# Attention in a one-core transformer block: the two heads or halves of a tile issued together on TensorE

## The chip, the cores and the metric

The program runs on one NeuronCore of one Trainium2 chip. The metric is the device time of one execution in microseconds. Three executions of the kernel before gave 3341.49, 3347.58 and 3352.87 us, median 3347.58.

## What is computed

One transformer block on two groups of tokens with shared weights: 1024 tokens (on a grid of 16 rows of 64) and 256 tokens. The reference, cut to what matters here:

```python
h = rms_norm(x, mix_norm_w)
qa, ka, va, qd, kd, vd = split(h @ w_in, 6)          # 6 x 512 columns
# neighbourhood attention: 8 heads of 64, window of 8 grid rows x 16 columns, learned bias
s = qg @ kg * 64**-0.5 + bias;  s = where(in_window, s, -inf)
ya = rms_norm(softmax(s) @ vg)                       # per head
# differential attention: 4 heads, q and k in two halves c of 64, v of 128, T5 bias
s = einsum('bqhcd,bkhcd->bhcqk', q, k) * 64**-0.5 + bias
p = softmax(s);  a = p[:, :, 0] - lam * p[:, :, 1]
yb = rms_norm(a @ v) * (1 - lambda_init)             # per head
x = x + concat(ya, yb) @ w_out
x = x + expert_choice_ffn(rms_norm(x))               # 16 experts, each token row routed
return rms_norm(x)
```

## The kernel before

The program has one written-out instruction order per engine; semaphores tie the engines together. Its stages, in order: normalisation and projection of V; four neighbourhood jobs (NA, two heads of 64 each); projection of V for the differential heads; four differential jobs (DF, one head with two halves of 64 each); the output projection; the router; sixteen experts; the final normalisation. Attention lies between 153 and 905 us of the profiled span.

A job works on the ten query tiles of 128 tokens (`TT`), tiles 0 to 7 of the long group and 8 and 9 of the short one. An NA tile has a window of 512 keys (t = 0, 1, 6, 7), 576 keys (t = 2 to 5, in two chunks of 288) or 256 keys (t = 8, 9); a DF tile has 1024 keys in two chunks of 512, or 256. A *unit* is one head or half of one tile, so there are twenty (`UNITS`) in a job. The two heads or halves sit in partitions 0 to 63 and 64 to 127 of `qk_h` and `qk_l`, which are the rounded value and the rest of q and k. The scores of one chunk of a unit are three matmuls over 64 rows (`three`, L542 to L544: high with high, low with high, high with low) into one half of the PSUM tensor `S`, which has one half for each of two units. Then:

- VectorE adds the bias, negates, writes the result to a slot of `E` in SBUF and takes its minimum (`bias_max`, L1215). It increments `scores_read`, which frees that half of `S`.
- ScalarE takes the exponential in place (`exps`, L937).
- In DF, VectorE then mixes the two halves (`mix`: a reciprocal L1257, a factor L1259, the mixing L1263).
- TensorE turns the blocks of 128 columns (`turn`, L537) into one of the two banks of `PT`, up to four blocks to a *fill*; a fill waits until the fill two before it is copied. ScalarE copies each fill to `PTs` (`turned_copy`, L924).
- TensorE multiplies with `Vj` (`na_values`, L598; `values`, L589) into `O` or `G`. In NA ScalarE copies that to `oTs` (L966), TensorE turns it once more, and ScalarE takes squares and copies it to `o_all` (`na_out`, L953 and L955). In DF ScalarE does it without the turn (`out_copy`, L932 and L933).

The order of NA on TensorE (L625 to L649) is by units: in step s the scores of unit s, the turns of unit s-2, the values of unit s-3, and in odd steps the turn of an output. The scores of a unit wait until the unit two before it has been read. ScalarE in step s: `na_out`, the copies of unit s-2, `oTs`, the exponential of unit s (L957 to L972). `w_round` (L880, ScalarE) and `w_lows` (L1136, VectorE) split the weights of the next job's projection after unit 8. Four projection rounds (`project`, rounded by `proj_round` and `proj_lows`) follow the attention of each job but the last DF job, with the last turns and values between them.

The order of DF on TensorE (`df_body`, L668) is by tiles: scores of both halves of tile t, values of t-2, turns of t-1, which wait for the mixing of t-1. VectorE: bias of half 0 of t, mixing of t-1, bias of half 1 of t. `E` has four slots, two for each of two tiles. GpSimd scales the finished heads and stores them (`heads`, `heads_scale`).

## Time and profile before

| | us |
|---|---|
| median of three runs | 3347.58 |
| span of the profiled execution | 3352.0 |
| its own time beside the span | not given apart from the span |
| TensorE busy (matmul) | 2967.7 (89%) |
| VectorE busy | 2059.2 (61%) |
| ScalarE busy | 1846.5 (55%) |
| GpSimd busy | 1355.1 (40%) |
| granted clock, mean of the span | 0.939 |

### The profile page before, as it was taken

How to read it: one execution, taken by the hardware profiler on the slowest of the kernel's cores; microseconds unless marked ns; L12 is line 12 of the kernel's file. 1: busy time of each engine (PE TensorE's matmuls, PEld its weight loads, DVE VectorE, ACT ScalarE, POOL GpSimd, SP SyncE). 2: the span in 40 equal slices, each digit the busy share in tenths (PEclk: the TensorE clock that was granted, in tenths of full speed). 3: DMA queues.
4: the chain of work that ended last, by engine and by line, in shares of the span. 5: the costliest groups of instructions: out<-in, count | busy, mean ns of one | idle time of the engine just before them, and what ended most of it. 6: DMA issues, size and time to landing. Idle time of an engine off the chain costs nothing.

```text
span 3352.0 us, 63730 instructions
## 1 busy us (share of the span) xinstructions
PE 2967.7 (89%) x23200; PEld 2709.3 (81%) x23200; DVE 2059.2 (61%) x2651; ACT 1846.5 (55%) x3280; POOL 1355.1 (40%) x1107
## 2 busy tenths in 40 slices
PE   3999999889698399898998999989989999899894
PEld 3877778777576298898988989889889898898894
DVE  3222223444533787786776867768768677687784
ACT  2144441444411176676665766756657667576674
POOL 1112211110211164564653745636447356374473
PEclk9999999999799599999999999999999999999997
DMA  6211100101235298998989989989899898898996
GB/s 157 75 25 32 45 32 21 33 28 31 83 126 176 65 298 252 274 271 250 289 256 246 296 250 281 264 243 303 250 265 278 254 278 263 246 300 248 274 273 215
DMA packets 790984, 657.24 MB, mean 196 GB/s; under 512 B 28311, under 2 KB 771863, under 8 KB 790263
## 3 DMA queue, kind: packets, MB, share of 16 engines
q1 hardware_dynamic: 778539, 608.52, 62.7%
q0 software_dynamic: 12240, 45.52, 5.2%
q8 instruction: 185, 3.03, 0.4%
q14 instruction: 20, 0.16, 0.0%
HBM read 618.58 MB, written 39.62 MB: 196 GB/s over the span
## 4 chain that ended last, share of the span: by engine, by line
PE 77%; issue 11%; DVE 5%; ACT 3%; DMA 2%; POOL 1%; DVEq 0%; SPq 0%; ACTq 0%; POOLq 0%
PE S L799 24%; PE S L802 11%; PE G L799 7%; PE S L542 6%; PE S L544 5%; PE S L543 5%; PE O L799 5%; PE PT L537 3%; PE G L802 3%; PE O L802 2%; DMA w_st<-in_w_in_dram 1%; PE O L598 1%; PE G L598 1%; ACT wh L1057 1%; DVE E L1215 1%
## 5 line engine op out<-in xcount | busy, mean ns | idle before, releaser
L1427 DVE TENSOR_TENSOR wl<-stg,wh 128x2048 bf16<-128x2048 f32 (+1 forms) x482 | 1260.3, 2617 | 323.0 <-ACT wh L1057 321.8
L799 PE MATMUL S<-X,wh 128*128 128x320 f32 x5632 | 940.3, 321 | 91.4 <-issue 86.7
L1057 ACT ACTIVATE wh<-stg 128x2048 fp32r<-128x2048 f32 (+1 forms) x482 | 1004.5, 2084 | 0.2
L799 PEld LDWEIGHTS S<-X,wh 128*128 128x128 f32 x5632 | 854.7, 194 | 98.9 <-issue 98.6
L1681 POOL TENSOR_TENSOR hx<-hh,hx 128x160 fp32r<-128x160 f32 x352 | 413.6, 1175 | 348.0 <-ACT hx L1089 347.7
L1683 POOL CAST hb<-hx 128x160 bf16<-128x160 f32 x352 | 549.0, 1560 | 0.0
L802 PE MATMUL S<-Xb,wl 128*128 128x160 bf16 x5632 | 454.7, 235 | 0.0
L802 PEld LDWEIGHTS S<-Xb,wl 128*128 128x128 bf16 x5632 | 385.0, 99 | 36.7 <-issue 1.4
L799 PE MATMUL O<-hx,wh 128*128 128x320 f32 x1408 | 229.8, 317 | 49.5 <-POOL hb L1683 49.5
L799 PEld LDWEIGHTS O<-hx,wh 128*128 128x128 f32 x1408 | 208.7, 190 | 54.0 <-POOL hx L1681 52.3
L799 PE MATMUL G<-hx,wh 128*128 128x320 f32 x1408 | 246.3, 336 | 0.0
L937 ACT ACTIVATE E<-E,nmax 128x1024 f32<-128x1024 f32 (+3 forms) x160 | 137.8, 861 | 176.7 <-DVE nmax L1215 176.7
L799 PEld LDWEIGHTS G<-hx,wh 128*128 128x128 f32 x1408 | 231.1, 209 | 0.7
L1575 POOL TENSOR_TENSOR ca<-lsum,half 128x20 f32<-128x20 f32 (+3 forms) x9 | 22.9, 2547 | 466.4 <-ACT o_all L933 342.9
L1663 POOL CAST Xb<-X 128x320 bf16<-128x320 f32 x68 | 109.7, 1625 | 211.5 <-ACT X L1047 211.5
L537 PE MATMUL PT<-identf,E 128*128 128x128 f32 x640 | 105.9, 300 | 94.5 <-DVE E L1175 49.6
L1074 ACT ACTIVATE glo<-S 128x160 f32<-128x160 f32 x352 | 87.4, 300 | 167.5 <-PE S L802 165.5
L537 PEld LDWEIGHTS PT<-identf,E 128*128 128x128 f32 x640 | 75.9, 150 | 120.6 <-issue 87.9
L1690 POOL DMA_INDIRECT residual<-ye,idx_c x16 | 25.9, 1619 | 361.0 <-ACT yes L1098 361.0
L1204 DVE SCALAR_TENSOR_TENSOR qk_l<-S,qk_h 128x1024 fp32r<-128x1024 f32 (+1 forms) x32 | 26.4, 825 | 214.4 <-ACT qk_h L912 214.4
L924 ACT ACTIVATE PTs<-PT 128x512 f32<-128x512 f32 (+2 forms) x184 | 87.0, 507 | 127.1 <-PE PT L537 126.8
L1462 DVE TENSOR_TENSOR hh<-sg,uu 128x160 f32<-128x160 f32 x352 | 114.9, 326 | 65.2 <-DVE uu L1457 61.3
(225 smaller groups left out, 4604.5 us busy)
## 6 DMA issues: line engine op xcount, KB each, us to landing
stg<-in_w_gate_dram SPq DMA_DIRECT2D x177, 1024.0 KB, 5.5
stg<-in_w_up_dram SPq DMA_DIRECT2D x177, 1024.0 KB, 5.6
stg<-in_w_down_dram SPq DMA_DIRECT2D x128, 1408.0 KB, 13.4
w_st<-in_w_in_dram SPq DMA_DIRECT2D x16, 512.0 KB
yt<-mixed SPq DMA_DIRECT2D x10, 512.0 KB, 3.8
residual<-x2t POOLq DMA_DIRECT2D x10, 512.0 KB, 4.4
ffn_in<-h2t POOLq DMA_DIRECT2D x10, 512.0 KB, 4.0
fin<-residual SPq DMA_DIRECT2D x10, 512.0 KB, 8.3
```

The lines of the kernel that those rows point to most:

```text
L537: mm = pe.transpose(PT[:, bank, m * P:(m + 1) * P], src(b), identf[:, :])
L542: pe.matmul(out, lhs_h, rhs_h, start=first, stop=False)
L543: pe.matmul(out, lhs_h, rhs_l, start=False, stop=False)
L544: return pe.matmul(out, lhs_l, rhs_h, start=False, stop=last)
L799: pe.matmul(out, w, x, start=first, stop=False, skip_group_check=True)
L802: return pe.matmul(out[:, 0:CT], w, x, start=False, stop=last, skip_group_check=True)
L937: act.activation(E[:, slot, 0:nk], E[:, slot, 0:nk], ACT.Exp, scale=-1.0, bias=nmax[:, col:col + 1], accum_out=lsum[:, job(j), t, c:c + 1] ...
L1057: act.activation(wh[:, kk % NCV, 0:w], stg[:, kk % NST, 0:w], ACT.Copy).then_inc(rounded, 1)
L1427: dve.tensor_tensor(wl[:, kk % NCV, 0:w], stg[:, kk % NST, 0:w], wh[:, kk % NCV, 0:w].bitcast(F32), ALU.subtract).then_inc(split, 1)
L1462: dve.tensor_tensor(hh[:, m, :], sg[:, m, :], uu[:, m, :], ALU.mult).then_inc(hidden_made, 1)
L1681: pool.tensor_tensor(hx[:, f, CT:2 * CT], hh[:, f % 2, :], hx[:, f, 0:CT].bitcast(F32), ALU.subtract).then_inc(hidden_ready, 1)
L1683: pool.tensor_copy(hb[:, f, :], hx[:, f, 0:CT].bitcast(F32)).then_inc(hidden_b, 1)
```

## The change

NA goes by tiles instead of units. On TensorE step s holds the scores of both heads of tile s, the values of both heads of tile s-2, the turns of both heads of tile s-1, and the turn of the output of tile s-3. Within the scores the three matmuls of a chunk alternate between the two heads (rows 0 to 63, rows 64 to 127), each head in its own half of `S`; within the values the blocks alternate between the two heads (columns 0 to 63, columns 64 to 127). The scores now wait until both heads of the tile before have been read. ScalarE in step s: both exponentials of tile s, `oTs` of tile s-2, `na_out` of tile s-4, the copies of tile s-1. `w_round` moves to the end of step 4, `w_lows` to after unit 11.

In DF the scores of the two halves alternate in the same way. The turns are those of tile t-2 and stand before the values, which are those of tile t-3. VectorE does both biases of tile t and then the mixing of t-1. A fifth slot `E5`, over the tables of NA, makes three slots for half 0, in turn by tile (`df_E`). The order of the projection rounds among the last turns and values changes with it.

```diff
     turns, outs, f = [], [], 0
-    for s in range(STEP):
-        if 2 <= s < UNITS + 2:
-            turns.append(f)
-            f += -(-na_blocks((s - 2) // 2) // 4)
-        if s % 2 and s >= 5:
+    for s in range(1, TT + 3):
+        if s <= TT:
+            for _ in range(2):
+                turns.append(f)
+                f += -(-na_blocks(s - 1) // 4)
+        if s >= 3:
             outs.append(f)
             f += 1
...
+    E5 = at("E5", [P, 1024], F32, 160 * K)
...
+    def df_E(t, c):
+        return E[:, 2 + t % 2, :] if c else (E[:, 0, :], E[:, 1, :], E5[:, :])[t % 3]
...
-            def scores(n, u, t, hf, k0, chunks):
-
-                pe.wait_ge(scores_read, n - 1)
-                rows = slice(64 * hf, 64 * hf + 64)
+            def scores(n, t, k0, chunks):
+
+                pe.wait_ge(scores_read, n)
                 q = slice(t * P, (t + 1) * P)
                 for at_, key, ln in chunks:
                     kk = slice(k0 + key, k0 + key + ln)
-                    mm = three(S[:, u % 2, at_:at_ + ln], qk_h[rows, 0, q], qk_l[rows, 0, q],
-                               qk_h[rows, 1, kk], qk_l[rows, 1, kk], True, True)
-                mm.then_inc(scores_ready, 1)
+                    for w, (qs, ks) in enumerate(((qk_h, qk_h), (qk_l, qk_h), (qk_h, qk_l))):
+                        for hf in range(2):
+                            rows = slice(64 * hf, 64 * hf + 64)
+                            mm = pe.matmul(S[:, hf, at_:at_ + ln], qs[rows, 0, q], ks[rows, 1, kk],
+                                           start=(w == 0), stop=(w == 2))
+                            if w == 2 and key + ln == chunks[-1][1] + chunks[-1][2]:
+                                mm.then_inc(scores_ready, 1)
 
             def values(o, par, fills_done, blocks, lhs, rhs, cols):
                 pe.wait_ge(turned_copied, fills_done)
...
-            def na_values(i, t, hf, fills_done, keys, kt0):
+            def na_values(i, t, fills_done, keys, kt0):
 
                 pe.wait_ge(turned_copied, fills_done)
                 pe.wait_ge(oT_copied, i * TT + (t + 1))
                 for b, n in enumerate(keys):
-                    mm = pe.matmul((O, G)[t % 2][64 * hf:64 * hf + 64, 0:P],
-                                   Vj[0:n, kt0 + b, 64 * hf:64 * hf + 64], PTs[0:n, hf, b, :],
-                                   start=(b == 0), stop=(b == len(keys) - 1))
-                mm.then_inc(out_ready, 1)
+                    for hf in range(2):
+                        mm = pe.matmul((O, G)[t % 2][64 * hf:64 * hf + 64, 0:P],
+                                       Vj[0:n, kt0 + b, 64 * hf:64 * hf + 64], PTs[0:n, hf, b, :],
+                                       start=(b == 0), stop=(b == len(keys) - 1))
+                        if b == len(keys) - 1:
+                            mm.then_inc(out_ready, 1)
 
 
...
                 n0, f0 = i * STEP + U_NA, i * NA_F
...
                         chunks = [(0, 0, 288), (512, 288, 288)] if inner else [(0, 0, nk)]
-                        scores(n0 + s, s, s // 2, s % 2, kt0 * P, chunks)
+                        scores(n0 + 2 * s, s, kt0 * P, chunks)
+                    elif s == TT:
+                        pe.wait_ge(w_split, i + (W_QKN + 1))
+                        project(n0 + UNITS, 0)
+                    elif s == TT + 1:
+                        project(n0 + UNITS, 1)
+                        project(n0 + UNITS, 2)
                     else:
-                        if s == UNITS:
-                            pe.wait_ge(w_split, i + (W_QKN + 1))
-                        project(n0 + UNITS, s - UNITS)
-                    if 2 <= s < UNITS + 2:
-                        u = s - 2
-                        pe.wait_ge(exp_done, i * UNITS + (u + 1))
-                        turn((f0, F_NA + NA_TURN[u]), list(range(na_blocks(u // 2))),
-                             lambda b: E[:, u % 4, b * P:(b + 1) * P])
-                    if 3 <= s < UNITS + 3:
-                        u = s - 3
-                        kt0, nk, _, _ = na_window(u // 2)
-                        if u == 0:
+                        project(n0 + UNITS, 3)
+                    if 2 <= s < TT + 2:
+                        t = s - 2
+                        kt0, nk, _, _ = na_window(t)
+                        if t == 0:
                             pe.wait_ge(vj_ready, i + 1)
-                        keys = [min(P, nk - b * P) for b in range(na_blocks(u // 2))]
-                        na_values(i, u // 2, u % 2, f0 + (F_NA + na_turned(u)), keys, kt0)
-                    if s % 2 and s >= 5:
-                        t = (s - 5) // 2
+                        keys = [min(P, nk - b * P) for b in range(na_blocks(t))]
+                        na_values(i, t, f0 + (F_NA + na_turned(2 * t + 1)), keys, kt0)
+                    if 1 <= s < TT + 1:
+                        for u in (2 * s - 2, 2 * s - 1):
+                            pe.wait_ge(exp_done, i * UNITS + (u + 1))
+                            turn((f0, F_NA + NA_TURN[u]), list(range(na_blocks(u // 2))),
+                                 lambda b: E[:, u % 4, b * P:(b + 1) * P])
+                    if s >= 3:
+                        t = s - 3
                         pe.wait_ge(oT_copied, i * TT + (t + 3))
                         turn((f0, F_NA + NA_OUT[t]), [t % 2], lambda b: oTs[:, b, :])
 
             v_project(W_VB, U_V1)
             v_project(W_VB + 1, U_V1 + TT)
 
-            def df_scores(n0, t, c):
+            def df_scores(n0, t):
                 k0, nk = df_keys(t)
-                scores(n0 + (2 * t + c), c, t, c, k0, [(a, a, min(512, nk - a)) for a in range(0, nk, 512)])
+                scores(n0 + 2 * t, t, k0, [(a, a, min(512, nk - a)) for a in range(0, nk, 512)])
 
             def df_turn(i, t):
                 pe.wait_ge(mixed, i * TT + (t + 1))
                 turn((i * DF_F, F_DF + df_fills(t)), list(range(df_keys(t)[1] // P)),
...
                         pe.wait_ge(vj_ready, i + (JOBS + 1))
                     if t >= 2:
-                        df_values(i, t - 2)
-                    if t >= 1:
-                        df_turn(i, t - 1)
+                        df_turn(i, t - 2)
+                    if t >= 3:
+                        df_values(i, t - 3)
                 if not last:
                     pe.wait_ge(w_split, i + (W_QKD + 1))
                     project(n0 + UNITS, 0)
+                df_turn(i, TT - 2)
+                df_values(i, TT - 3)
+                if not last:
+                    project(n0 + UNITS, 1)
+                    project(n0 + UNITS, 2)
                 df_turn(i, TT - 1)
                 df_values(i, TT - 2)
                 if not last:
-                    project(n0 + UNITS, 1)
-                    project(n0 + UNITS, 2)
+                    project(n0 + UNITS, 3)
                 df_values(i, TT - 1)
-                if not last:
-                    project(n0 + UNITS, 3)
 
 
             with pe.Fori(0, JOBS - 1) as i:
...
-                        na_out((s - 6) // 2)
-                    if 2 <= s < UNITS + 2:
-                        u = s - 2
-                        turned_copy(f0, F_NA + NA_TURN[u], i * UNITS + u, u % 2, na_blocks(u // 2))
-                    if s % 2 and s >= 5:
-                        t = (s - 5) // 2
+                for s in range(TT + 4):
+                    if s < TT:
+                        exps(i, n0 + 2 * s, E[:, 2 * s % 4, :], na_window(s)[1], 2 * s, s, 0)
+                        exps(i, n0 + 2 * s + 1, E[:, (2 * s + 1) % 4, :], na_window(s)[1], 2 * s + 1, s, 1)
+                    elif s == TT:
+                        proj_round(n0 + UNITS, 0)
+                    elif s == TT + 1:
+                        proj_round(n0 + UNITS, 1)
+                        proj_round(n0 + UNITS, 2)
+                    elif s == TT + 2:
+                        proj_round(n0 + UNITS, 3)
+                    if 2 <= s < TT + 2:
+                        t = s - 2
                         act.wait_ge(out_ready, i * UNITS + (2 * t + 4))
                         act.activation(oTs[:, t % 2, :], (O, G)[t % 2][:, 0:P], ACT.Copy).then_inc(oT_copied, 1)
-                    if s < UNITS:
-                        exps(i, n0 + s, s % 4, na_window(s // 2)[1], s, s // 2, s % 2)
-                    elif s < STEP:
-                        proj_round(n0 + UNITS, s - UNITS)
-                    if s == 8:
+                    if 4 <= s < TT + 4:
...
+                    if s == 4:
                         w_round(W_QKN, i)
 
...
 
                 for t in range(TT):
                     nk = df_keys(t)[1]
+                    for c in range(2):
+                        exps(i, n0 + (2 * t + c), df_E(t, c), nk, 2 * t + c, t, c)
                     if t >= 2:
                         tcopy(t - 2)
-                    exps(i, n0 + 2 * t, 2 * (t % 2), nk, 2 * t, t, 0)
                     if t == 3:
                         act.wait_ge(heads_normed, i + (JOBS + 1))
                     if t >= 3:
                         ocopy(t - 3)
-                    exps(i, n0 + (2 * t + 1), 2 * (t % 2) + 1, nk, 2 * t + 1, t, 1)
...
-                    if s == 8:
+                    if s == 11:
...
+                    if t >= 3:
+                        dve.wait_ge(turned, i * DF_F + (F_DF + df_fills(t - 2)))
+                    elif t == 0:
+                        dve.wait_ge(turned, i * DF_F + F_DF)
+                    if t >= 2:
+                        dve.wait_ge(mixed, i * TT + (t - 1))
                     for c in range(2):
-                        if t >= 2:
-                            dve.wait_ge(turned, i * DF_F + (F_DF + df_fills(t - 1)))
-                        else:
-                            dve.wait_ge(turned, i * DF_F + (F_DF - DF_F + df_fills(TT + t - 1)))
-                        slot = 2 * (t % 2) + c
                         bias_max(n0 + (2 * t + c), c, S[:, c, 0:nk],
                                  BT[:, (TPR - 1) * P - tl * P:(TPR - 1) * P - tl * P + nk],
-                                 E[:, slot, 0:nk], 2 * t + c)
-                        if c == 0 and t >= 1:
-                            mix(i, t - 1)
+                                 df_E(t, c)[:, 0:nk], 2 * t + c)
+                    if t >= 1:
+                        mix(i, t - 1)
```

TensorE in NA, in the middle of the four tiles of 576 keys: before, the end of one unit's scores, then turns and values, each of one head (the line in brackets names the semaphores that an instruction waits for; `S<-qk_h 128x288` is a chunk of scores, `PT<-identf,E` a turn, `O<-PTs,Vj` values).

```order
L542 MATMUL S<-qk_h 128x288
L543 MATMUL S<-qk_l,qk_h 128x288
L544 MATMUL S<-qk_h,qk_l 128x288
L636 REGISTER_ALU
L533 REGISTER_ALU [waits exp_done]
L537 MATMUL PT<-identf,E 128x128 [waits turned_copied]
L537 MATMUL PT<-identf,E 128x128 x3
L533 REGISTER_ALU
L537 MATMUL PT<-identf,E 128x128 [waits turned_copied]
L598 MATMUL O<-PTs,Vj 64x128 [waits oT_copied,turned_copied]
L598 MATMUL O<-PTs,Vj 64x128 x4
L648 REGISTER_ALU
```

The same place in the change (L588 is the scores' matmul, L607 the values').

```order
L588 MATMUL S<-qk_h 128x288 [waits scores_read]
L588 MATMUL S<-qk_h 128x288
L588 MATMUL S<-qk_h,qk_l 128x288 x2
L588 MATMUL S<-qk_l,qk_h 128x288 x2
L588 MATMUL S<-qk_h 128x288 x2
L588 MATMUL S<-qk_h,qk_l 128x288 x2
L588 MATMUL S<-qk_l,qk_h 128x288 x2
L603 REGISTER_ALU
L607 MATMUL O<-PTs,Vj 64x128 [waits oT_copied,turned_copied]
L607 MATMUL O<-PTs,Vj 64x128 x9
L657 REGISTER_ALU
L542 MATMUL PT<-identf,E 128x128 [waits turned_copied,exp_done]
```

The scores of a tile are twelve matmuls in a row with one wait, the values ten, and the turns stand behind them.

ScalarE in NA, one unit before: output of an earlier tile, the two copies of a turned unit, the exponential.

```order
L950 REGISTER_ALU [waits turned_copied]
L953 ACTIVATE junk,sso<-PT 128x64 [waits turned]
L953 ACTIVATE junk,sso<-PT 128x64
L955 ACTIVATE o_all<-PT 128x128
L923 REGISTER_ALU [waits out_ready]
L924 ACTIVATE PTs<-PT 128x512 [waits turned]
L923 REGISTER_ALU
L924 ACTIVATE PTs<-PT 128x128 [waits turned]
L936 REGISTER_ALU
L937 ISA [waits scores_read]
L937 ACTIVATE E,lsum<-E,nmax 128x576
```

The change, from the second exponential of a tile on (L952 is the exponential, L986 `oTs`, L968 and L970 the output, L939 the copies).

```order
L951 REGISTER_ALU
L952 ISA [waits scores_read]
L952 ACTIVATE E,lsum<-E,nmax 128x576
L986 ACTIVATE oTs<-G 128x128 [waits out_ready]
L965 REGISTER_ALU [waits turned_copied]
L968 ACTIVATE junk,sso<-PT 128x64 [waits turned]
L968 ACTIVATE junk,sso<-PT 128x64
L970 ACTIVATE o_all<-PT 128x128
L938 REGISTER_ALU [waits out_ready]
L939 ACTIVATE PTs<-PT 128x512 [waits turned]
L938 REGISTER_ALU
L939 ACTIVATE PTs<-PT 128x128 [waits turned]
```

The copies have moved from before the exponential to behind both exponentials, `oTs` and the output.

VectorE in DF, before: the bias of half 0 of tile t, the mixing of tile t-1 (L1257 to L1263), the wait for the bias of half 1.

```order
L1215 ISA E,nmax<-S,BT 128x1024 [waits scores_ready]
L1215 ISA nmax 128x1
L1256 REGISTER_ALU
L1257 ISA [waits exp_done]
L1257 RECIPROCAL rl_88<-lsum 128x1
L145 REGISTER_ALU
L1259 ISA [waits dve_own]
L1259 TENSOR_SCALAR cf<-rl_88,lsum,lam_s 128x1
L145 REGISTER_ALU
L1263 SCALAR_TENSOR_TENSOR E<-E,cf 128x1024 [waits dve_own]
L1213 REGISTER_ALU [waits turned]
L1215 ISA E,nmax<-S,BT 128x1024 [waits scores_ready]
```

The change, from the wait ahead of tile 2 on (L1236 is the bias, L1278 and L1280 lead to the mixing).

```order
L1234 REGISTER_ALU [waits mixed]
L1236 ISA E_65,nmax<-S,BT 128x1024 [waits scores_ready]
L1236 ISA nmax 128x1
L1234 REGISTER_ALU
L1236 ISA E,nmax<-S,BT 128x1024 [waits scores_ready]
L1236 ISA nmax 128x1
L1277 REGISTER_ALU
L1278 ISA [waits exp_done]
L1278 RECIPROCAL rl_89<-lsum 128x1
L146 REGISTER_ALU
L1280 ISA [waits dve_own]
L1280 TENSOR_SCALAR cf<-rl_89,lsum,lam_s 128x1
```

Both biases stand ahead of the mixing; the wait on `mixed` is new.

## Rows read from the trace of the kernel before

**Rows 1.** Of the page: the chain that ended last, by engine

```profile
PE 77%; issue 11%; DVE 5%; ACT 3%; DMA 2%; POOL 1%; DVEq 0%; SPq 0%; ACTq 0%; POOLq 0%
```

**Rows 2.** Sums by stretch: start and end, length, busy time (instructions), clock, DMA

```profile
sum 226.40, PE 219.03 PEld 159.56 DVE 66.57 ACT 137.88 POOL 42.90; mean PE 54.76 PEld 39.89 DVE 16.64 ACT 34.47 POOL 10.72
...
564.00:649.95 85.95, 75.87 (x459) 63.34 (x457) 41.70 (x76) 38.92 (x92) 1.48 (x1) 0.96 0.08 25
649.95:741.20 91.25, 79.90 (x458) 67.05 (x457) 44.44 (x76) 39.41 (x93) 11.49 (x10) 0.91 0.10 29
741.20:831.40 90.20, 79.08 (x458) 66.35 (x457) 44.43 (x76) 39.29 (x93) 11.44 (x10) 0.92 0.06 18
831.40:905.00 73.60, 55.09 (x313) 45.79 (x312) 49.40 (x78) 42.16 (x90) 17.00 (x17) 0.84 0.23 75
```

**Rows 3.** Timeline, TensorE in an NA tile: start, busy us, engine, line, operation

```profile
264.36 0.40 PE L542 MATMUL S<-qk_h 64*128 64x288 f32 x1
264.60 0.29 PE L543 MATMUL S<-qk_l,qk_h 64*128 64x288 f32 x1
264.73 0.29 PE L544 MATMUL S<-qk_h,qk_l 64*128 64x288 f32 x1
267.42 0.33 PE L537 MATMUL PT<-identf,oTs 128*128 128x128 f32 x1
267.68 0.40 PE L542 MATMUL S<-qk_h 64*128 64x288 f32 x1
```

**Rows 4.** Timeline, VectorE and ScalarE in the same stretch (in brackets: idle, and its releaser)

```profile
262.55 0.76 DVE L1215 CUSTOM_DVE_ANT_0 E<-S,TI 128x576 f32<-128x576 f32 x1 [2.55 <-PE S L544]
264.39 1.91 ACT L880 ACTIVATE w_h<-w_st 128x2048 fp32r<-128x2048 f32 x1
266.33 2.29 DVE L1136 TENSOR_TENSOR w_l<-w_st,w_h 128x2048 fp32r<-128x2048 f32 x1 [3.02 <-ACT w_h L880]
269.42 0.78 ACT L937 ACTIVATE E<-E,nmax 128x576 f32<-128x576 f32 x1 [2.31 <-DVE nmax L1215]
270.74 0.81 ACT L924 ACTIVATE PTs<-PT 128x512 f32<-128x512 f32 x2
271.45 0.77 ACT L937 ACTIVATE E<-E,nmax 128x576 f32<-128x576 f32 x1
```

**Rows 5.** Timeline, a DF tile: TensorE and VectorE

```profile
606.97 0.50 PE L542 MATMUL S<-qk_h 64*128 64x512 f32 x1
607.31 0.40 PE L543 MATMUL S<-qk_l,qk_h 64*128 64x512 f32 x1
607.55 0.61 PE L542 MATMUL S<-qk_h 64*128 64x512 f32 x2
608.81 1.22 DVE L1215 CUSTOM_DVE_ANT_0 E<-S,BT 128x1024 f32<-128x1024 f32 x1 [1.85 <-PE S L544]
608.82 0.39 PE L544 MATMUL S<-qk_h,qk_l 64*128 64x512 f32 x1
610.57 1.28 DVE L1263 SCALAR_TENSOR_TENSOR E<-E,cf 128x1024 f32<-128x1024 f32 x1
611.98 1.09 PE L537 MATMUL PT<-identf,E 128*128 128x128 f32 x8 [0.57 <-DVE E L1263]
```

**Rows 6.** Timeline, TensorE at the scores of the first short DF tile

```profile
613.00 0.43 PE L542 MATMUL S<-qk_h 64*128 64x256 f32 x2
```

**Rows 7.** Two slices round the rounding of an NA job's weights

```profile
178.00:181.00 3.00, 1.40 (x11) 1.04 (x11) 1.26 (x4) 2.29 (x10) 0.00 (x0) 1.00 0.00 0
181.00:184.00 3.00, 3.00 (x13) 2.23 (x11) 0.00 (x0) 0.60 (x2) 0.00 (x0) 0.51 0.00 0
```

**Rows 8.** Timeline, VectorE in the first tiles of the second DF job

```profile
658.51 2.17 DVE L1263 SCALAR_TENSOR_TENSOR E<-E,cf 128x1024 f32<-128x1024 f32 x1
667.23 1.22 DVE L1215 CUSTOM_DVE_ANT_0 E<-S,BT 128x1024 f32<-128x1024 f32 x1
```

**Rows 9.** Timeline, the first projection matmul behind the first DF job

```profile
621.07 0.47 PE L542 MATMUL S<-hT_h,w_h 128*128 128x512 f32 x1
```

More of the change, by code:

```diff
@@ L955, in na_out @@
                     act.activation(o_all[:, t, :], PT[:, bank, 0:P], ACT.Copy).then_inc(turned_copied, 1)
-                for s in range(STEP + 1):
-                    if s % 2 == 0 and s >= 6:
-                        na_out((s - 6) // 2)
-                    if 2 <= s < UNITS + 2:
-                        u = s - 2
-                        turned_copy(f0, F_NA + NA_TURN[u], i * UNITS + u, u % 2, na_blocks(u // 2))
-                    if s % 2 and s >= 5:
-                        t = (s - 5) // 2
+                for s in range(TT + 4):
+                    if s < TT:
+                        exps(i, n0 + 2 * s, E[:, 2 * s % 4, :], na_window(s)[1], 2 * s, s, 0)
[9 more added lines that the diff above has]
+                        t = s - 2
                         act.wait_ge(out_ready, i * UNITS + (2 * t + 4))
                         act.activation(oTs[:, t % 2, :], (O, G)[t % 2][:, 0:P], ACT.Copy).then_inc(oT_copied, 1)
-                    if s < UNITS:
-                        exps(i, n0 + s, s % 4, na_window(s // 2)[1], s, s // 2, s % 2)
-                    elif s < STEP:
-                        proj_round(n0 + UNITS, s - UNITS)
-                    if s == 8:
+                    if 4 <= s < TT + 4:
+                        na_out(s - 4)
+                    if 1 <= s < TT + 1:
+                        for u in (2 * s - 2, 2 * s - 1):
+                            turned_copy(f0, F_NA + NA_TURN[u], i * UNITS + u, u % 2, na_blocks(u // 2))
+                    if s == 4:
                         w_round(W_QKN, i)
@@ L1002, in df_body @@
                         w_round(NW + t // 2)
+                if not last:
+                    proj_round(n0 + UNITS, 0)
                 tcopy(TT - 2)
@@ L1009, in df_body @@
                 if not last:
-                    proj_round(n0 + UNITS, 1)
-                    proj_round(n0 + UNITS, 2)
+                    proj_round(n0 + UNITS, 3)
                 ocopy(TT - 1)
-                if not last:
-                    proj_round(n0 + UNITS, 3)
             with act.Fori(0, JOBS - 1) as i:
```

22 lines of the change are left out of this document (11 added, 11 removed).

## The prediction, written before the changed kernel ran

> **What bounds the kernel now.** I read the page first. TensorE is busy in 89% of the span, and the chain that ended last is 77% TensorE [rows 1]; but most of that is the experts' stage, which the change leaves alone. So I cut out the two attention stages. The four stretches in which the neighbourhood jobs (NA) attend take 226.4 us together, 56.6 each, the four differential jobs (DF, the projections between them included) 341.0 us [rows 2]. The change can touch only these 567 us.
>
> Next the timeline of a steady NA tile of 576 keys. TensorE goes from the scores of one head (64 rows) to turns, to values with 128 rows, to values with 64 rows and to scores again, with some 0.17 us lost at each change of shape and no other gap. A head with the turn of an output takes 264.36 to 267.68 = 3.32 us, one without it 0.26 less (267.42 to 267.68): 6.38 us a tile [rows 3]. ScalarE and VectorE wait there. NA is bound by TensorE.
>
> In DF it is otherwise. From scores to scores a tile takes 606.97 to 613.00 = 6.03 us [rows 5, 6], and the rows form a ring: scores, bias and maximum of half 0 (608.81), reciprocal, factor and mixing of the tile before (610.57, 1.28 us), its turns (611.98, which waited 0.57 us on that mixing), scores again. DF is bound by this ring, and no engine is full in it.
>
> **Do the two halves run together?** The diff rests on it, and before already shows it. In the two short tiles the scores of both halves stand right behind each other, and the two first matmuls show as one row of x2 that spans 0.43 us, where one alone lasts 0.38 [rows 6]. With 512 columns half 1's first matmul starts at 607.55, beside half 0's third, and before half 0's fourth (the x2 row at 607.55 spans 0.61 us) [rows 5]. Its twelve matmuls take 606.97 to 609.21 = 2.24 us. A step beside the other half is as long as alone, 0.23 to 0.24 us (607.31 to 607.55). So rows 0-63 and 64-127 overlap at full speed. Alternating, DF scores need 0.34 + 4 x 0.23 + 0.39 = 1.65 us, a gain of only 0.6. For NA scores and for the column groups of the values no row of before shows a pair: values in between nothing (20 records a tile at 0.11 us, the step of the turns, of which eight span 1.09 us [rows 5]) and half (10 slots).
>
> The Trainium skill, TensorE: Matmul & The Clock Gate, section on packing small matmuls, says that matmuls start strictly in program order. The rows at 607.55 say otherwise; by the page the scores of before would be longer by some 0.5 us, and the change worth that much more on the tiles where TensorE sets the time. I go by the rows, and no term uses it.
>
> **NA, the change part by part.** Scores of a tile: twelve matmuls become six slots; four changes of shape a tile instead of nine, at 0.17 us. TensorE's own work of a 576-key tile falls from 6.38 to about 1.0 + 1.4 + 1.4 = 3.8 us if values pair, 4.9 if not. But now `scores` waits until both halves of the tile before are read, and ScalarE does both exponentials of tile s before the copies of tile s-1, on which turns of s-1 wait, behind which stand the scores of s+1. That is a closed ring. Walked with its rows [rows 3, 4], from the start of scores(s): half 0 ready at 0.24 + 4 x 0.13 + 0.29 = 1.05; bias 0.19 later, 0.76 long: 2.00; ScalarE 0.13 later, two exponentials of 0.77: 3.67; `oTs` 0.16: 3.83; output of tile s-4 0.55 (269.42 to 270.74 less one exponential): 4.38; copy of the first fill 0.6 (both fills 0.71): 4.98; only then the second head's four turns (0.65): 5.6; their copy 0.6: 6.25; out turn and change to scores 0.3: 6.6 us. Against 6.38 that is a loss. Whether values pair matters 0.2 us to it, they lie beside ScalarE's part. The same walk gives 5.0 us for a 512-key tile in the place of some 5.3, and 3.9 and 3.5 for the two 256-key tiles. The first three tiles lack parts of the ring and take 2.5, 2.5 and 4.2, the fourth 6.0. Tiles 0 to 9: 2.5 + 2.5 + 4.2 + 6.0 + 6.6 + 6.6 + 6.25 + 5.0 + 3.9 + 3.5 = 47.1 us, and 1.3 for the second-head turns that now wait behind round 0 of the projection: 48.4.
>
> Before spends 56.6. Two things in it go. The weight rounding (1.91 us on ScalarE, then 2.29 on VectorE after a 3.02 us wait) stands in front of copies that TensorE needs [rows 4]; moved to the end of ScalarE's tile 4 it lies in 2.2 us in which ScalarE waits for bias(5), and the VectorE half after unit 11 lies in a wait for scores. Its cost: TensorE busy 1.40 of 3 us at 178, then the granted clock at 0.51 in 181-184, 1.2 GHz [rows 7]: some 2.5 us of stall and 3.4 of half clock. What is late next is the ring. And it starts slower: with TensorE under half busy in the first 5 us I expect a spell at half clock in each job, 3 us. I add 1 us for steps between engines that I left out: 52.4 a job, 209.6 in all, **-17 us**. Bounds: no spell, nothing left out, -33; half clock in all of it (scores 0.8 us longer, and the values, twice as long, stand in front of the first turn: ring 8.6, 2 us more on eight tiles, 2 in front): 66 a job, +38.
>
> The page TensorEngine Tiling (Array Packing) of the Trainium skill, section PSUM Bottleneck, warns that tiling speeds up TensorE but not the emptying of PSUM. The trace agrees for NA: 3.8 us of matmul in a ring of 6.6. By the page's other figure, up to 2x for halves of 64, NA would gain some 80 us; by the ring it can't.
>
> **DF.** The ring is cut: turns of t-2 need a mixing that ended 0.3 us or more before, thanks to the third buffer of `E`. What is late next is TensorE itself: scores 1.5, change 0.2, eight turns 0.9, sixteen value records 1.8, change 0.2 = 4.6 us. VectorE needs 2 x 1.15 + 1.81 = 4.1, ScalarE 2 x 1.15 + 1.0 + 0.5 = 3.8, and from scores to both biases read it is 1.84 + 2.31 = 4.15: all below 4.6. Start of a job: bias(2) came 667.23 - 649.95 = 17.3 us after the first scores [rows 2, 8]. Now 4.15 (scores and both biases), 2.67 (`Vj`), 2.31 (two biases): 9.1; exponential 1.28 and rounding 1.9: 12.3, beside the mixing; `w_lows` 2.3: 14.6. Then 4.15 and five times 4.6 to bias(8), less 0.85: scores(8) at 40.9, with 2 us for a spell at half clock 42.9. Two short tiles 7.5: projection at 50.4. Its part lasted 621.07 to 649.95 = 28.9 us [rows 2, 9]; turn(8) and values(7) stand in it now as well, 2.05: 30.9. Sum 81.3, in job 0, whose `Vj` copy is 1.9 us shorter, 79.4. Against 85.95, 91.25 and 90.20 [rows 2] that is -6.6, -10.0, -8.9. The last job keeps four roundings: a tile with one lasts 9.2 (ScalarE's rounding comes behind both exponentials, copy and output: 2.3 + 1.28 + 1.0 + 0.5 + 1.9 + 2.2), one without 4.6: 14.6 + 4.15 + 3 x 9.2 + 2 x 4.6 - 0.85 + 7.5 + 3.8 for what is left = 66.0 against 73.6, -7.6. Sum -33. VectorE's mixing takes 2.17 instead of 1.28 us while GpSimd works [rows 8] and may now stand in the way more often; I take 1.5 us a job off: **-27 us**. Bounds: -38 (no half clock) and -12 (TensorE's cycle at 5.3 instead of 4.6).
>
> Nothing else moves: the instructions outside these loops stand as before, the experts' stage among them; the end of the last job hangs on GpSimd's two passes over the heads, as before.
>
> **Sum.** 3352.0 - 17 - 27 = 3308 us for an execution like the profiled one, whose span is 3352.0; nothing beyond it is known of that execution's own time. The median of the three runs shown is 3347.58, 4.4 less: 3304 us.
>
> **Rivals.**
> 1. The clock in steady NA. TensorE's columns fill 4.7 of 6.4 us now, then 3.0 of 6.6. A slice with a long gap is followed by 0.51 [rows 7], which speaks for it. Against: the gaps of the new ring are spread, and both heads' columns still pass. If it swings between the levels, +5 us a job: NA +3, total -24: 3324 us. Chance 0.25.
> 2. Slower than before, by one mechanism: the ring keeps NA at half clock all through. +38 - 27 = +11: 3359 us. It decides from a mean granted clock in NA under about 0.6 (where NA's loss, 7 us a job, eats DF's gain). Before has 0.84 to 0.96 in the DF jobs [rows 2]. Chance 0.07.
> 3. The change doesn't do what it says: alternate heads with a wait or a tag between them don't pair, scores last as long as one after the other. NA's ring is 0.8 longer on eight tiles: -17 + 26 = +9. DF's cycle is 1.2 longer on five: -27 + 24 = -3. Together +6: 3354 us. The x2 row at 613.00 [rows 6] speaks against. Chance 0.06.
> The forecast keeps 0.62, its own range 3285 to 3318.
>
> **Numbers.** Range 3278 (both lower bounds make -71, 3277) to 3336 (rival 1 with DF at its poor bound). A measurement tells 0.3%, 10 us, from no change. Faster by over 0.3%: the forecast, rival 1 nearly all: 0.85. Within: part of rival 1 and rival 3: 0.08. Slower: 0.07.
>
> **What would show it.** NA stretches of 50 to 54 us, inner tiles of 6.4 to 6.8 with TensorE waiting on copies (`PT` on ScalarE L939), ScalarE without the 3 us wait round the rounding; granted clock 0.9 or more. DF tiles at 4.6 to 4.8, TensorE without waits on mixing; DF jobs near 81 and the last 66. It is wrong if NA tiles last under 6 us (a wait that I placed in the ring is not there), if DF tiles stay over 5.3, or if PEclk in NA falls below 0.8.

## The result: 14 us slower, and the profile after

The changed kernel takes 3365.86 us (median of six runs, 3363.68 to 3371.97) against 3351.86 of before (six runs, 3341.49 to 3357.72): ratio 1.0047, 95% interval 1.0031 to 1.0063. The forecast was 3304.0, range 3278 to 3336. The time is outside it, on the side that got a chance of 0.07, and not by the mechanism of that rival.

One execution of e5 (11210.75 us) and one of the kernel before beside e5, e6 and e7 (4249.48 us) were slow with unchanged code, so all figures and ratios below are of the others; the median of e5 with its slow one is 3191.84, from which the expectations of e8, e9 and e10 start.

The attention stages did what was forecast. First the sum over the four NA stretches of the changed kernel, which answers to the sum of [rows 2] (226.40 us), then its DF jobs, which answer to the four others (341.0 us; 304.83 now):

```profile
148.49:197.91 49.42, 36.70 (x312) 25.78 (x312) 15.61 (x42) 31.70 (x104) 0.00 (x0) 0.90 0.01 3
...
sum 198.71, PE 146.85 PEld 103.89 DVE 62.45 ACT 128.93 POOL 42.85; mean PE 36.71 PEld 25.97 DVE 15.61 ACT 32.23 POOL 10.71
```

```profile
541.17:620.42 79.25, 68.73 (x457) 57.58 (x457) 41.63 (x76) 38.63 (x93) 0.00 (x0) 0.96 0.09 27
620.42:701.19 80.77, 70.13 (x456) 58.56 (x456) 43.01 (x76) 38.79 (x94) 11.03 (x9) 0.92 0.11 33
701.19:780.83 79.64, 68.45 (x456) 57.28 (x457) 43.47 (x76) 38.80 (x95) 11.04 (x9) 0.94 0.06 21
780.83:846.00 65.17, 45.55 (x276) 36.99 (x277) 46.12 (x76) 38.95 (x80) 13.43 (x14) 0.75 0.25 84
```

The NA stretches end at the first projection matmul, and more of the last tiles' turns and values now stands behind it: the parts between the stretches and up to DF take 9.5 us more (193.97 against 184.45), so of the 27.7 us in the stretches 18.2 are left.

The experts' first matmul starts at 1099.8 us, where before it started at 1154.7: 54.9 us earlier (4.6 of them are the stage ahead of NA, whose time differs from run to run with unchanged code). Yet the span is 10.9 us longer, so the experts give back 66. From the first expert's first matmul to the sixteenth's the changed kernel takes 139.3 us an expert, before 135.2; 15 x 4.1 = 62 us of it lie there.

The view of the groups, TensorE's weight loads from 1100 us on, has the place. The first group is the load for the first half of an expert (columns: line, engine, operation, names, shapes, count, then busy time and mean ns, then the idle time before it and what ended it). Before:

```profile
L799 PEld LDWEIGHTS S<-X,wh 128*128 128x128 f32 x5632 | 854.7, 194 | 98.9 <-issue 98.6
```

and after, the same 5632 loads:

```profile
L814 PEld LDWEIGHTS S<-X,wh 128*128 128x128 f32 x5632 | 858.0, 194 | 158.8 <-issue 158.4
```

The instructions take the same time; 60 us more are idle, and "issue" says that the profile shows nothing that the engine waited for. On the timeline of TensorE this stands where the experts' loop (`pe.Fori(0, NE)`) goes round. Before:

```profile
1418.92 0.27 PE L861 MATMUL PT<-identf,yTe 128*32 128x128 f32 x1
1425.08 1.43 PE L799 MATMUL S<-X,wh 128*128 128x320 f32 x4 [5.88 <-issue]
```

After:

```profile
1507.45 0.27 PE L876 MATMUL PT<-identf,yTe 128*32 128x128 f32 x1
1513.58 0.63 PE L814 MATMUL S<-X,wh 128*128 128x320 f32 x1 [5.85 <-issue]
1517.41 1.97 PE L814 MATMUL S<-X,wh 128*128 128x320 f32 x6 [3.21 <-issue]
```

Both have a hole of 5.9 us at the branch. The changed kernel has a second one of 3.2 us (up to 4.2 at other turns) behind a single matmul. For the queue that carries instructions the page of before has:

```profile
q8 instruction: 185, 3.03, 0.4%
```

and after:

```profile
q8 instruction: 200, 3.28, 0.4%
```

Fifteen packets more (of 3.03 MB / 185 = 16384 bytes) for fifteen turns. In 1419 to 1430 of before that queue has 2 packets, in 1507 to 1522 of after 3:

```profile
q8 instruction: 3, 0.05, 1.3%
```

The times of these packets in the two traces tie the holes to them. In before one starts at 1422.23 and has landed at 1423.32, and TensorE goes on at 1425.08. In after one has landed at 1511.88, and TensorE goes on at 1513.58; the next starts only at 1515.18 and has landed at 1516.16, and the second hole ends at 1517.41. It is so at every turn: the first hole ends 1.7 to 1.9 us behind a landing, the second 1.2 to 1.6 us behind the next one.

The stalls cost more than their own length through the clock. In slices of 3 us (columns as in [rows 2]; the number behind the brackets is the granted clock) before has the clock at 0.50 in one slice and at 0.61 in the next:

```profile
1425.00:1428.00 3.00, 2.92 (x11) 2.93 (x12) 0.60 (x1) 0.00 (x0) 0.00 (x0) 0.50 0.87 171
1428.00:1431.00 3.00, 3.00 (x24) 2.80 (x22) 0.00 (x0) 0.00 (x0) 0.53 (x4) 0.61 0.86 281
```

After has it at 0.50 in four slices running and at 0.78 in the one behind:

```profile
1507.00:1510.00 3.00, 0.66 (x4) 0.36 (x4) 0.02 (x1) 2.82 (x6) 0.58 (x1) 0.95 0.90 273
1510.00:1513.00 3.00, 0.00 (x0) 0.00 (x0) 1.16 (x1) 1.81 (x1) 2.39 (x2) 0.50 0.76 138
1513.00:1516.00 3.00, 0.63 (x1) 0.29 (x1) 1.13 (x1) 0.00 (x0) 0.00 (x0) 0.50 0.96 174
1516.00:1519.00 3.00, 1.58 (x6) 1.59 (x7) 0.00 (x0) 0.00 (x0) 0.53 (x4) 0.50 0.88 281
1519.00:1522.00 3.00, 3.00 (x14) 2.80 (x13) 0.00 (x0) 0.00 (x0) 0.00 (x0) 0.50 0.20 67
```

No number in the experts' code changed. What changed is its place. The built program of TensorE has the head of this loop at instruction 6883 before and at 6854 after: register arithmetic and waits that stood once per unit now stand once per tile, 19 fewer in the NA loop and 10 in the DF loop. An instruction is 64 bytes in the built program, so a packet is a piece of 256; the longest program here, e5 below, has 42589 instructions, 166.4 such pieces, and its queue moved 166 packets. The experts' loop has 2283 instructions. The NA loop has 1081 before and 1062 after, the DF loop 982 and 972. From the stall behind the sixth instruction of the loop I read that a border of pieces lies there: the head sits 6 instructions ahead of a piece's end. In before it sits 23 behind a piece's beginning.

### The profile page after: what moved, and what is told of

It reads as the page before. It is cut to its first block, busy times and chain, and to the rows that moved or that the text cites. A ratio compares the mean times of both kernels' runs of the same rounds, so it can differ in the third digit from the quotient of the medians.

```text
span 3362.9 us, 63649 instructions
## 1 busy us (share of the span) xinstructions
PE 2875.7 (86%) x23200; PEld 2633.1 (78%) x23200; DVE 2048.9 (61%) x2651; ACT 1842.8 (55%) x3280; POOL 1356.4 (40%) x1107
## 4 chain that ended last, share of the span: by engine, by line
PE 75%; issue 12%; DVE 5%; ACT 5%; DMA 2%; POOL 1%; DVEq 0%; SPq 0%; ACTq 0%; POOLq 0%
PE S L814 24%; PE S L817 11%; PE G L814 7%; PE O L814 5%; PE S L547 4%; PE S L548 4%; PE S L549 4%; PE G L817 3%; PE S L588 3%; PE PT L542 3%; PE O L817 2%; DVE E L1236 1%; DMA w_st<-in_w_in_dram 1%; ACT wh L1078 1%; ACT PTs L939 1%
## 5 line engine op out<-in xcount | busy, mean ns | idle before, releaser
L952 ACT ACTIVATE E<-E,nmax 128x1024 f32<-128x1024 f32 (+3 forms) x160 | 136.9, 856 | 188.2 <-DVE nmax L1236 188.2
L1476 DVE TENSOR_TENSOR gg<-S,glo 128x160 f32<-128x160 f32 x352 | 96.0, 312 | 152.1 <-ACT glo L1095 152.1
```

The lines of the kernel that those rows point to most:

```text
L952: act.activation(dst[:, 0:nk], dst[:, 0:nk], ACT.Exp, scale=-1.0, bias=nmax[:, col:col + 1], accum_out=lsum[:, job(j), t, c:c + 1].rearran ...
```

## Experiments

**Theory F** (for fetch): at the branch TensorE waits for the piece with the loop's head; if that piece ends a few instructions later, it waits again for the next. **Rival G**: the experts pay for something the attention stages left behind, such as their phase against the weight loads or the clock.

### The same code at another place

e1 puts 29 instructions in front of the experts' loop of the changed kernel, e2 puts 227 in front of that of before (23 + 227 = 250, the place in the piece that the change gave it):

```diff
+            for _ in range(2 * 29):                # two waits make one instruction
+                pe.wait_ge(ident_ready, 1)         # met long ago
             with pe.Fori(0, NE) as e:
```

> Theory F (position of the experts' loop in TensorE's program): the program of before reaches the head of that loop 29 instructions later than the changed one; the loop spans one piece of 256 instructions (16384 bytes, as the instruction fetches show) less there. 29 instructions (each two waits already met) put ahead of the loop bring that back: an expert takes 135.6 us again instead of 139.6, the second idle stretch behind the loop's branch goes, the fetches fall from 200 to 185, and the time is 3363 - 16 x 4.1 = about 3298 us. Rival G (the experts pay for something that the attention stages changed: their phase against the weight loads, the buffers, the clock that they inherit): the experts stay at 139.6 us and the time at 3363 us, within 5.

> The kernel before with 227 instructions of the same kind ahead of the experts' loop: its head then lies where the changed kernel has it, 256 instructions (one piece) further on. Theory F: attention as before (experts start at about 1154 us, plus about 10 for the added waits), an expert 139.6 us instead of 135.6, 200 fetches or one more, and a time of 3352 + 65 + 10 = about 3425 us. Rival G: experts at 135.6 us and 3352 to 3365 us.

e1: 3300.36 us (3297.91 to 3302.40), ratio to before 0.9843 (0.9823 to 0.9863), 135.1 us an expert, 185 packets. Adding 29 instructions makes the changed kernel 65 us faster. Its group row is that of before again:

```profile
L814 PEld LDWEIGHTS S<-X,wh 128*128 128x128 f32 x5632 | 855.0, 194 | 98.4 <-issue 98.0
```

e2: 3440.56 us, ratio 1.0261 (1.0238 to 1.0284), 139.1 us an expert, 201 packets, so with nothing of the change the same loss appears. It is 15 us above what I had expected, 11 of them because I had put the added waits at 10 us: the experts start at 1175.8 instead of 1154.7, 21 us later. Its row:

```profile
L799 PEld LDWEIGHTS S<-X,wh 128*128 128x128 f32 x5632 | 857.5, 194 | 179.3 <-issue 178.9
```

G has fallen.

### Each half of the change alone

e3 has the NA hunks of the diff and the DF stage of before, e4 the reverse. (The old `scores` stays beside the new one as `scores_one`.)

```diff
e3:  NA loop -> scores(n0 + 2 * s, s, kt0 * P, chunks)          DF -> scores_one(...)
e4:  NA loop -> scores_one(n0 + s, s, s // 2, s % 2, ...)       DF -> scores(n0 + 2 * t, ...)
```

> Only the neighbourhood heads' part of the change. TensorE's program is 19 instructions shorter ahead of the experts' loop. Theory F: its head then still lies in the same piece as before (only 19 and 10 together pass the border), so the experts keep 135.6 us; the neighbourhood stages give 4 x 5 us, and the time is about 3332 us. Rival G, if this part is the one that carries over: the experts at 139.6 us and 3332 + 65 = 3397 us.

> Only the differential heads' part of the change. TensorE's program is 10 instructions shorter ahead of the experts' loop. Theory F: same piece as before, experts at 135.6 us; the four stages give 6.6, 10.5, 10.2 and 10.6 us as the changed kernel's trace shows them, and the time is about 3352 - 38 = 3314 us, faster than the whole change. Rival G: experts at 139.6 us, 3314 + 65 = 3379 us.

e3: 3335.43 us, ratio 0.9946 (0.9931 to 0.9962). e4: 3312.97 us, ratio 0.9881 (0.9861 to 0.9901). Both have 185 packets and 135.1 us an expert. Each half of the change is a gain; only together do they shorten the program by 29 and pass the border at 23. The heads lie 4 and 13 instructions behind the piece's beginning here.

### How near to the border

e6 has 242 such instructions, placed where TensorE is idle (ahead of the wait for `sel_ready`), so that 20 instructions of the loop are left in the first piece instead of 6.

> The changed kernel with 242 waits already met, put where TensorE idles through the selection of the tokens, so that the head of the experts' loop lies 20 instructions ahead of a piece's end instead of 6. Theory F as a matter of timing (the second fetch takes about 3.9 us from the first one's landing, and what is left of the first piece runs meanwhile): the second idle stretch shrinks by the 14 more instructions, 7 matmuls at about 0.3 us, from 3.8 to about 1.7 us; an expert takes about 137.5 us and the time is about 3330 us, with 200 or 201 fetches. Theory F as a matter of count (a fetch more costs its 4 us wherever the head lies): 3363 us with the same 139.6 us an expert. Rival G: 3363 us.

3335.80 us, ratio 0.9960 (0.9948 to 0.9972), 137.1 us an expert, 201 packets. The timeline of TensorE at a turn:

```profile
1508.25 2.50 PE L816 MATMUL S<-X,wh 128*128 128x320 f32 x8 [5.75 <-issue]
1512.55 1.70 PE L816 MATMUL S<-X,wh 128*128 128x320 f32 x5 [1.80 <-issue]
```

Eight matmuls run ahead of the second hole instead of one, and it is 1.80 us long (1.0 to 2.1 at other turns). The border had been placed from one stall alone. 14 instructions more are 7 matmuls (a load and a matmul each), and 1 became 8, so the place is right to such a pair. And it is timing, not the packet itself: the same number of packets costs less when there is work to cover the fetch.

### No turn at all

```diff
-            with pe.Fori(0, NE) as e:
+            for e in range(NE):                    # written out, TensorE alone
```

e5 does this to the changed kernel, e8 to that of before.

> The changed kernel with the experts' loop of TensorE written out 16 times, so that its program has no branch there (the other engines keep their loops). Theory F: both idle stretches behind each turn (5.9 and 3.8 us) and the half-clock spell after them go; against e1_after_pad29 (3300 us), which has the 5.9 us alone, that is at least 15 x 5.9 = 88 us if TensorE is the only bound, so 3212 us or less. Rival H: the weight transfers, whose engines are busy 0.94 of the experts' stage in e1_after_pad29, end last as soon as the turns are gone; then at most 0.06 x 2170 = 130 us are to be had and some of the 88 us will show as waits for weights: 3215 to 3260 us. Rival I: straight code of 2.7 MB is fetched no faster than it is run and TensorE waits for each piece: 3300 us or more.

> The kernel before with the experts' loop of TensorE written out, as in e5_no_loop. Theory F: where no branch is left, nothing of the experts' stage depends on the program's length ahead of it; written out, the loop gives before what it gave e1_after_pad29, 3300 - 3192 = 108 us, so 3352 - 108 = 3244 us, and the change itself, read between this and e5_no_loop, is worth -52 us. Rival G (something else of the change costs in the experts' stage, masked by the shift so far): the distance to e5_no_loop is nearer the +14 us of the two kernels as they stand, 3178 to 3220 us.

e5: 3189.23 us, ratio 0.9528 (0.9499 to 0.9557). This version beats both kernels: by 4.7% the one before, by 5.2% the changed one. An expert takes 128.0 us. e8: 3243.28 us, ratio 0.9691 (0.9675 to 0.9707), 127.9 us an expert. The change is worth 3189.23 - 3243.28 = -54.1 us where code placement is out of play. In e5 both holes are gone:

```profile
L814 PEld LDWEIGHTS S<-X,wh 128*128 128x128 f32 x5626 | 828.4, 188 | 10.6 <-issue 9.4
```

Rival I fell: 2.7 MB of straight code (166 packets) arrive in time. Rival H was half right: its range, 3215 to 3260 us, did not come, but in the stretch from 1160 to 3060 the DMA engines are now at 0.99 (0.91 after), so this stage seems to have little more to give:

```profile
1160.00:3060.00 1900.00, 1844.87 (x16298) 1762.93 (x16296) 1480.60 (x1690) 1344.04 (x2075) 1077.64 (x828) 0.98 0.99 282
```

### What in the change carries its gain

e7 is e1 with the alternation taken out of scores and values; the loops over halves go outside. e9 is e5 with a wait between the halves' scores. e10 is e5 with the turns one step earlier.

```diff
e7
-                    for w, (qs, ks) in enumerate(...):
-                        for hf in range(2):
+                    for hf in range(2):
+                        for w, (qs, ks) in enumerate(...):
e9
+                for hf in range(2):
+                    if hf:
+                        pe.wait_ge(scores_ready, n + 1)
e10
-                    if t >= 2:
-                        df_turn(i, t - 2)
                     if t >= 3:
                         df_values(i, t - 3)
+                    if t >= 1:
+                        df_turn(i, t - 1)
```

> e1_after_pad29 with the same order of stages, but the two heads or halves one after the other within a tile's scores (three matmuls of half 0, then three of half 1) and values. If the overlap of two row groups carries the gain: a differential tile has 12 score matmuls, in pairs at 0.43 us against 0.43 each (the row of 613.00 us before), 2.6 us a tile more, so the differential tiles are back at about 6 us less what the order gave, and the time is 3300 + 35 = 3335 us or more. If the later turns and values carry it: 3300 to 3310 us.

> e5_no_loop with TensorE made to wait for half 0's scores of a tile (its own count of finished scores) before it starts half 1's, in both attention stages; order of stages, work and all else as changed. Theory O (the gain is the overlap of the two halves on their row groups, which the engine finds by itself as long as no wait stands between them): a differential tile has 12 score matmuls of 512 columns, in six pairs of 0.23 us each in e7_no_alternation; one after the other that is six more times 0.23 and about 0.3 us for the wait, so 4.5 + 1.7 = 6.2 us a tile, the whole differential gain gone, and with the neighbourhood's 5 us a stage 3192 + 40 to 55 = 3232 to 3247 us. Theory S (turns and values issued later carry it): at most 3192 to 3205 us.

> e5_no_loop with TensorE's order in the differential tiles put back by one step in the turns alone: behind the scores of tile t come the values of t-3 and then the turns of t-1 (the change has the turns of t-2). The pairs of halves stay. If the late turns carry a part of their own: the turns of t-1 need the mixing of t-1, which VectorE does behind both row maxima of tile t; in e5_no_loop the scores of a tile start at 643.0 and the mixing ends at 649.0 us, the turns take 1.1 us, so the next scores start 7.1 us on instead of 4.5, at some 5 long tiles in each of 4 stages and half as much in the 3 short ones: 3192 + 45 to 70 = 3237 to 3262 us. If the overlap alone carries the gain: 3192 to 3200 us.

e7: 3300.07 us, ratio 0.9851 (0.9831 to 0.9872), the same as e1's 3300.36. My "if the overlap carries it, 3335" was wrong in its premise: taking out the alternation does not take out the overlap. The DF scores of e7, three matmuls of half 0 and then three of half 1 in program order for each chunk:

```profile
574.38 0.51 PE L588 MATMUL S<-qk_h 64*128 64x512 f32 x2
574.72 0.40 PE L588 MATMUL S<-qk_h,qk_l 64*128 64x512 f32 x2
574.96 0.40 PE L588 MATMUL S<-qk_l,qk_h 64*128 64x512 f32 x2
```

They run in pairs all the same. A pair spans 0.40 us, as one does alone in e9, and the pairs follow each other at 0.23 to 0.24 us. Half 1's first matmul is in the first row, ahead of half 0's second at 574.72, though two of half 0's stand before it in the program. The Trainium skill, TensorE: Matmul & The Clock Gate, Part 3 on packing small matmuls, calls the start of matmuls strict program order; by that rule e7 would have lost most of the pairs. The trace does not agree, and neither does the time. What the halves need is that no wait stands between them.

e9: 3320.76 us, 132 us above e5, where I had expected 40 to 55. From the first DF scores to the first expert it takes 50 us more than e5, from the first NA scores to the first DF scores 85. The DF tile is as worked out, scores at 663.99 to turns at 667.30, and tiles 6.2 us apart (row maxima at 659.7, 665.8, 672.0, 678.0):

```profile
664.33 0.39 PE L590 MATMUL S<-qk_h,qk_l 64*128 64x512 f32 x1
...
665.71 0.50 PE L590 MATMUL S<-qk_h 64*128 64x512 f32 x1
```

NA is what I missed. Its stretches last 71 us (49 in the changed kernel) at a granted clock of 0.56 to 0.59:

```profile
146.09:217.59 71.50, 65.90 (x312) 46.27 (x312) 16.40 (x42) 34.10 (x104) 0.00 (x0) 0.56 0.02 5
250.83:321.44 70.61, 64.56 (x311) 45.17 (x312) 16.40 (x42) 34.75 (x110) 14.33 (x9) 0.59 0.04 10
```

That is the mechanism of the prediction's rival 2, a ring at half clock all through NA. The changed kernel stays clear of it, with 0.86 to 0.90, and so does e5, with 0.79 in the first NA stretch and 0.86 to 0.93 in the others. Scores one half after the other, half 1 starting 1.3 us behind half 0 where the clock is full, are enough to fall in. The rows do not say how much of the 71 us is the longer ring and how much the clock, since each holds up the other.

e10: 3265.28 us, 76 us above e5, where the expectation had 45 to 70. So the late turns are needed too: pairs alone give 3265. TensorE stands behind ScalarE's copies and VectorE's mixing there (waits of TensorE in 620 to 760: in total, times, longest):

```profile
PE PT L542 <- ACT PTs L938: 17.2, 7, 4.5
PE PT L542 <- DVE E L1283: 12.5, 2, 6.4
```

Against e8 (3243.28, before's own order without the loop) e10 is even 22 us slower: half of the new order is worse than none.

## Why the prediction was wrong

**The step that failed** is the last of its parts: "Nothing else moves: the instructions outside these loops stand as before, the experts' stage among them". The instructions do stand as before, but 29 places further forward in TensorE's program, and the head of the experts' loop passed the border of a fetched piece. That costs +4.1 us an expert, 62 us over fifteen turns; e1 (take the shift away) and e2 (give it to before) show it in both directions. The chain of [rows 1] has "issue 11%", of which I had made nothing. It holds the 5.9 us of each turn (the chain of before has 5.88 us of it from 1419.19 on), and that was the largest sum to be had here: e8 takes before down by 3.1%, about 104 us, by this alone. No rival named it.

**Without that step the forecast holds.** e1 has the changed kernel's attention and before's place of the loop: 3300.36 us, where the prediction had 3304.0. That it is so near is in part luck: the pair of traces gained 18 us in NA for 17 forecast and 32 in DF for 27, and inside NA two deviations cancel (below). The range had a slip as well: rival 1 with DF at its poor bound makes 3347.6 + 3 - 12 = 3339, not 3336, which changes nothing here.

**NA, -17 forecast.** From the first NA scores to the first DF scores: 410.9 us before, 392.7 after, -18.3. That flatters, as other runs with before's NA code (e2, e4, e8) have 405.6 to 410.2 and others with the new one 392.9 to 395.8, so about -14. The stretches themselves came out at 49.4 to 50.3 us a job, below the 52.4 forecast and its sign of 50 to 54; the 9.5 us behind them took that back. The walked ring was right in kind and size. Scores to scores takes 171.33 to 177.98 = 6.65 us for a 576-key tile (6.6 forecast), and TensorE waits on ScalarE's copies as it said:

```profile
171.07 0.33 PE L542 MATMUL PT<-identf,oTs 128*128 128x128 f32 x1 [0.58 <-ACT PTs L939]
171.33 0.40 PE L588 MATMUL S<-qk_h 64*128 64x288 f32 x2
...
177.98 0.50 PE L588 MATMUL S<-qk_h 64*128 64x512 f32 x2
```

The values pair, at least in part: 20 of them span 1.46 us where each alone after the other would take 20 x 0.11 = 2.2. A spell at half clock came in each job, as allowed for (clock 0.86 to 0.90). The sign "PEclk in NA below 0.8" was a poor one: e5's first stretch has 0.79 and lasts 49.4 us like the others.

**DF, -27 forecast out of a sum of -33.** Jobs of 79.25, 80.77 and 79.64 (forecast 79.4, 81.3, 81.3), the tile at 4.47 us (4.6 forecast), TensorE without a hole in it. Scores to scores in the changed kernel, with the turns and values between:

```profile
572.34 0.51 PE L588 MATMUL S<-qk_h 64*128 64x512 f32 x2
...
573.99 1.11 PE L542 MATMUL PT<-identf,E 128*128 128x128 f32 x8
574.93 1.95 PE L597 MATMUL G<-Vj,PTs 128*128 128x128 f32 x16
576.81 0.50 PE L588 MATMUL S<-qk_h 64*128 64x512 f32 x2
```

From the first DF scores to the first expert before has 590.6 us and the changed kernel 558.6: -32. e3 and e8 (DF as before) have 595.9 and 597.9, e1, e4, e5 and e7 (DF as changed) 558 to 560; the means of the two groups, these two traces among them, are 35 apart. The 1.5 us a job taken off for VectorE beside GpSimd was not needed, and the sum of -33 was the better number.

**Rival 1** (clock swings in NA, +5 us a job) didn't come as a cost: the jobs are 2 to 3 us under the forecast. **Rival 3** (halves don't pair) fell by the x2 rows above. Of the "change does what it says": the alternation written into the diff does nothing measurable (e7 against e1, 0.3 us); its pairs come from issuing both halves behind one wait.

**Left open.** The 5.9 us at the branch are, in every trace with the loop, 2.4 to 3.2 us from the last matmul to the start of a packet, about 1.1 for the packet and 1.7 to 2.0 until TensorE goes on. What sets the first and the last of these, and how far ahead of use the next piece is asked for in straight code, isn't settled; no run was made for it. That the shorter loops fetch nothing at their turns is a reading of two loops (the queue of instructions moved nothing between 240 and 515 us of before, while the NA loop of 1081 instructions ran three more times), not a threshold.

## What to carry to other kernels

When code changes ahead of a long loop, a shift by itself is part of the change: look at the idle time "issue" at the loop's turn, count the instruction queue's packets before and after, and time the change once with the shift filled up or with the loop written out, or a gain of 1.6% reads as a loss of 0.4%. If a loop's turn shows a hole of "issue" and the clock falls behind it, try that loop written out on that engine before tuning anything else. For overlap between row groups, take the waits away between the two halves; the order of their instructions need not alternate.

## What the runs showed of the hardware that was not expected

- Instructions come in packets of 16384 bytes. A loop of 2283 instructions on TensorE fetches ten or eleven of them at every round, with a stall of 5.3 to 6.1 us at the branch, and a second of 1.0 to 2.1 us when 20 instructions of the loop's head are left in its first piece (e6) and of 3.2 to 4.2 us when 6 are (after, e2). Each stall ends 1.2 to 2.0 us behind the landing of a packet. With 233, 243 and 252 left (e1, e4, e3) there is none.
- The price is more than the stall. The two holes of a turn are 9 us, but writing the loop out saves the changed kernel 3365.86 - 3189.23 = 177 us, 11.8 us a turn; the rest goes with the slices at clock 0.50 behind the hole and with the weight transfers, which pause (DMA at 0.20 in 1519 to 1522). How it splits between these was not measured.
- Matmuls on rows 0-63 and 64-127 overlap at full speed when three of one group stand ahead of three of the other in the program: a pair spans 0.40 us, as one alone does (e7, e9). TensorE starts an instruction of the other row group ahead of earlier ones.
- One wait between the halves of the scores took the granted clock of the four NA stretches from 0.79 to 0.93 (e5) down to 0.54 to 0.60 (e9), and a stretch from 49 to 71 us.
